# Gated attention, rms norm of a head's output: one fp32 product with ones, against two fp32r products with the high and low part of the sum

## What is computed

```python
o = o_intra + jnp.moveaxis(o_inter, 0, 1)
o = o * lax.rsqrt(jnp.mean(o * o, axis=-1, keepdims=True) + NORM_EPS)
o = o.reshape(B, L, D_INNER) * gn_g
return (o.astype(x.dtype) * jax.nn.silu(z)) @ w_out
```

## Time and profile before

| | |
|---|---|
| median of 3 runs | 1708.46 us |
| lowest, highest | 1706.99, 1709.57 us |
| the profiled execution's own time | 1711.55 us |
| its span | 1709.7 us |
| mean granted TensorE clock | 0.997 |
| PE busy | 1689.3 us (99%), 7852 matmuls |
| DVE, ACT, POOL busy | 960.2 (56%), 610.3 (36%), 976.4 us (57%) |

### The profile page before, as it was taken

How to read it: one execution, slowest core, us unless ns; L and a number is a source line. 1 busy time by engine, 2 the same in 40 slices (tenths; PEclk the granted TensorE clock), 3 DMA queues, 4 the chain that set the end, 5 groups by cost and what they waited for, 6 DMA issues and landing times.

```text
span 1709.7 us, 22074 instructions
## 1 busy us (share of the span) xinstructions
PE 1689.3 (99%) x7852; PEld 1404.5 (82%) x7852; DVE 960.2 (56%) x1637; ACT 610.3 (36%) x1160; POOL 976.4 (57%) x595
## 2 busy tenths in 40 slices
PE   9999999999999999998999999999999999999998
PEld 7788788888888888887888888888888888888887
DVE  6878422155642554255857444437657967775244
ACT  4455321243312222043733322322524037765022
POOL 6656566665667666665655466446564663333654
PEclk9999999999999999998999999999999999999999
DMA  5212232322233322323222222222232221111222
GB/s 205 85 58 79 87 99 98 99 87 91 95 101 108 99 98 93 104 99 102 84 89 72 77 96 87 83 77 87 86 99 81 90 96 50 50 50 62 87 89 84
DMA packets 52424, 152.26 MB, mean 89 GB/s; under 512 B 11376, under 2 KB 12528, under 8 KB 52336
## 3 DMA queue, kind: packets, MB, share of 16 engines
q1 hardware_dynamic: 51472, 149.50, 26.5%
q10 hardware_dynamic: 864, 1.57, 0.3%
HBM read 148.95 MB, written 2.10 MB: 88 GB/s over the span
## 4 chain that ended last, share of the span: by engine, by line
PE 94%; DVE 4%; issue 1%; ACT 1%; DMA 0%; SPq 0%; DVEq 0%; POOL 0%; ACTq 0%; POOLq 0%
PE bank L867 27%; PE bank L869 27%; PE bank L868 27%; DVE fx L2540 1%; PE bank L1714 1%; PE bank L1312 1%; PE bank L1313 1%; PE bank L1316 1%; PE bank L1557 1%; PE bank L1554 1%; PE bank L1553 1%; PE bank L1051 1%; PE bank L905 1%; PE bank L891 0%; DVE fx L2745 0%
## 5 line engine op out<-in xcount | busy, mean ns | idle before, releaser
L782 POOL TENSOR_SCALAR w_hi<-raw 128x1024 fp32r<-128x1024 f32 (+2 forms) x276 | 287.2, 1040 | 654.0 <-issue 482.9
L784 POOL TENSOR_TENSOR w_lo<-raw,w_hi 128x1024 fp32r<-128x1024 f32 (+2 forms) x276 | 646.7, 2343 | 23.1
L867 PE MATMUL bank<-op_hi,w_hi 128*128 128x512 f32 x964 | 381.8, 396 | 2.5 <-POOL w_lo L772 1.0
L869 PE MATMUL bank<-op_hi,w_lo 128*128 128x512 f32 x964 | 375.8, 390 | 0.0
L868 PE MATMUL bank<-op_lo,w_hi 128*128 128x512 f32 x964 | 375.5, 390 | 0.0
L867 PE MATMUL bank<-r,w_hi 128*128 128x512 f32 x856 | 339.2, 396 | 0.6 <-POOL w_lo L784 0.5
L869 PE MATMUL bank<-r,w_lo 128*128 128x512 f32 x856 | 333.9, 390 | 0.0
L868 PE MATMUL bank<-r,w_hi 128*128 128x512 f32 x856 | 333.7, 390 | 0.0
L867 PEld LDWEIGHTS bank<-op_hi,w_hi 128*128 128x128 f32 x964 | 181.4, 188 | 40.7 <-issue 2.0
L869 PEld LDWEIGHTS bank<-op_hi,w_lo 128*128 128x128 f32 x964 | 180.9, 188 | 38.0
L868 PEld LDWEIGHTS bank<-op_lo,w_hi 128*128 128x128 f32 x964 | 181.3, 188 | 36.3 <-issue 1.0
(11 more groups left out here) (306 smaller groups left out, 2346.5 us busy)
## 6 DMA issues: line engine op xcount, KB each, us to landing
raw<-in_weights SPq DMA_DIRECT2D x266, 512.0 KB, 3.3
out<-h SPq DMA_DIRECT2D x8, 256.0 KB, 2.0
h<-in_x SPq DMA_DIRECT2D x3, 512.0 KB, 8.3
raw<-in_weights SPq DMA_DIRECT2D x8, 192.0 KB, 2.4
raw<-in_weights SPq DMA_DIRECT2D x8, 128.0 KB, 2.7
cst<-in_consts SPq DMA_DIRECT2D x1, 832.0 KB, 11.4
raw<-in_weights SPq DMA_DIRECT2D x3, 256.0 KB, 3.2
rope_cos<-in_p ACTq DMA_DIRECT2D x3, 256.0 KB, 3.6
```

Of the source, the lines that this page charges most:

```text
L782: pool.tensor_scalar(hi, raw[:, r, at:w], 1.0, 0.0, ALU.mult, ALU.add).then_inc(hi_ready, 1)
L784: pool.tensor_tensor(lo, raw[:, r, at:w], hi.bitcast(F32), ALU.subtract).then_inc(split_ready, 1)
L867: pe.matmul(o, ah, bh, start=start, stop=False, skip_group_check=skip)
L869: return pe.matmul(o, al, bh, start=False, stop=stop, skip_group_check=skip)
```

## The change

After the last square is added up, ACT rounds the sum `acc` to fp32r (`oth`, into `total_hi`, which is tile 2 of `fx`) and DVE subtracts that from `acc` (`otl`, into `total_lo`, tile 0 of `fx`). `gla_sum` then makes two fp32r products with an fp32r matrix of ones, one with each part, added up in bank 7, instead of one fp32 product with `acc`. It waits for `otl` in place of `oacc2`. The matrix of ones in fp32r is made once by a copy of 128 x 128 on DVE, at the start of the stage `gla_a` (step `ones`), in the place of the constant `tri`, which nothing reads. On ACT `oth` stands behind the squares and the exponentials of the next head and ahead of `z3`, `z0` (heads 1 and 2) or right ahead of `osqrt` (heads 0 and 3). On DVE `otl` stands behind `on3` and `on0`, in every head.

```diff
+        total = nc.alloc_sbuf_tensor_at("total", [P, 3 * T], F32R, offset=nc.sbuf_base)
         fx = sb("fx", [P, 12, T], F32)
...
+        ones_r = nc.alloc_sbuf_tensor_at("ones_r", [P, P], F32R, offset=nc.sbuf_base + 4 * C0["tri"])[:, :]
         cst = sb("cst", [P, CONSTS], F32)
...
+        total_hi, total_lo = total[:, 2 * T:3 * T], total[:, 0:T]
...
-            gla_act += gla_decays_act(1, n) * inner + gla_names(p, *["z3", "z0"] * inner, "osqrt", "oh0", "oh3")
+            gla_act += gla_decays_act(1, n) * inner + gla_names(p, "oth", *["z3", "z0"] * inner, "osqrt", "oh0", "oh3")
...
-            gla_dve += gla_names(p, "on3", "on0", *["on1", "on2"] * first, "ors", "oz0", "oz3", "ol0", "ol3", *["on1"] * (not first), "oz1",
+            gla_dve += gla_names(p, "on3", "on0", "otl", *["on1", "on2"] * first, "ors", "oz0", "oz3", "ol0", "ol3", *["on1"] * (not first), "oz1",
...
             def gla_sum(p):
-                pe.wait_ge(d.sem, d.at(f"oacc2_{p}"))
                 pe.wait_ge(d.sem, d.at(f"on3_{p}"))
-                z.done(full_sum(7), f"osum_{p}")
+                pe.wait_ge(d.sem, d.at(f"otl_{p}"))
+                pe.matmul(ps[7][:, :], ones_r, total_hi, start=True, stop=False)
+                z.done(pe.matmul(ps[7][:, :], ones_r, total_lo, start=False, stop=True), f"osum_{p}")
...
+            def gla_total_high(p):
+                act.wait_ge(d.sem, d.at(f"oacc{GLA_BLOCKS[-1]}_{p}"))
+                hi(a, f"oth_{p}", total_hi, acc)
...
                 gla_squares(p)
                 if inner:
                     gla_decays(1, p + 1)
+                gla_total_high(p)
+                if inner:
                     gla_gate(3, p)
                     gla_gate(0, p)
                 gla_root(p)
...
+            d.done(dve.tensor_copy(ones_r, ones), "ones")
             d.done(dve.tensor_tensor_scan(later_keys, ones, ident, 1.0, ALU.mult, ALU.subtract), "later")
...
+            def gla_total_low(p):
+                sync(a, f"oth_{p}")
+                lo(d, f"otl_{p}", total_lo, acc, total_hi)
...
                 gla_gated(3, p)
                 gla_gated(0, p)
+                gla_total_low(p)
                 if first:
                     gla_gated(1, p)
                     gla_gated(2, p)
```

More of the change, by code:

```diff
@@ L458, in build @@
         stage("gla_a", 1, ["ah0", "ah1"] + [f"ab{m}" for m in M8] + ["ex0", "ex1", "ln0", "ln1"] + [f"{a}{m}" for a in ("ex", "ln") for m in range(2, KD)],
-              ["later", "sm", "al"] + [f"mn{m}" for m in M8] + QK, [f"a{m}" for m in range(KD - 1)])
+              ["ones", "later", "sm", "al"] + [f"mn{m}" for m in M8] + QK, [f"a{m}" for m in range(KD - 1)])
         def gla_names(p, *names):
```

## The result

The changed kernel takes 1714.96 us, median of 6 runs (1713.94 to 1715.64), the kernel before 1707.96 us in the 6 runs beside them. The ratio is 1.0037 (95% interval 1.0027 to 1.0047): slower by about 6.3 us (by the medians alone it would be 7.0). The profiled execution took 1715.55 us with a span of 1713.8, against 1711.55 and 1709.7 before.

A forecast was written before the change was run, and what follows sets the result against it. PE (TensorE), busy 99% of the span, was taken to bound the kernel. Savings of 0.41 us in heads 0 and 3 and losses of 1.95 in heads 1 and 2 gave +3.1: 1708.46 to 1711.6 us, range 1708.9 to 1716.7.

The forecast's parts named there:

- the mechanism that I gave 0.72: Four heads' sums: 0.41 us saved in heads 0 and 3, 1.95 us lost in heads 1 and 2, +3.1 us.
- one fall of 5.1 us: Behind a stall in head 1 or 2, PE's clock halves for 10.3 us and loses 5.1 us: 1716.7 us.
- The price of the products: Each head's sum on PE: two fp32r products take 0.46 us against 0.87 for fp32, saving 0.41 us without a wait.
- The step that laid the chain bare: Heads 1 and 2: PE's sum waits through gate 0, `z0`, `on0`, `otl`; stall about 2.4 us, net 1.95 us later.
- Where nothing should be late: `oth` off the chain, 2.0 us of cover in heads 0 and 3, nothing new late behind the stalls.
- The copy of ones: On DVE ahead of `later`: well under 1 us, costing nothing because DVE stands idle 5.92 us there.
- rival (b): Stalls in heads 1 and 2 halve PE's clock: 1716.7 us for one head, 1721.9 for both; chance 0.11.
- five waits of up to 1.1 us: Earlier PE waits in the trace that left the clock at 1.00, cited against a fall of the clock.
- The one fall in the trace: At 781.5 us PE's clock went from 1.00 to 0.50 for 10.3 us, after 3.3 us with 1.80 busy.
- The condition that I had set: Heads 1 and 2: the clock falls once 2.1 us without any product on PE is enough.
- Rival (a): All four heads' waits stay hidden: 0.41 us saved in each, -1.6 us, 1706.8 us; chance 0.08.
- Rival (c): The pair of products costs what one fp32 product did, 0.87 us: +4.7 us, 1713.2 us; chance 0.09.

The follow-up runs named there:

- The filled wait: Changed kernel with nine unread products of 128x512 in each of PE's two waits, heads 1 and 2: 1711.59 us, ratio 1.0018 to the kernel before.
- the fp32 sum: Changed kernel, waits and added steps included, but with one fp32 product as the sum in place of the pair: 1715.41 us, ratio 1.0044 to the kernel before.
- the one of one head: Changed kernel with the low part `otl` ahead of `on0` on DVE in head 2 alone: 1711.22 us, ratio 1.0013 to the kernel before.
- the first experiment: Changed kernel with the low part `otl` ahead of `on0` on DVE in every head: 1707.59 us, ratio 0.9993 to the kernel before.
- the sum behind gate 1: Changed kernel with PE's sum moved from ahead of gate 1 to behind it in heads 1 and 2: 1711.02 us, ratio 1.0014 to the kernel before.

## Why the prediction was right and wrong

The time lay in the range, and slower was the sign, but the mechanism that I gave 0.72 was only half of it: 3.1 us forecast, 6.3 measured. That the range held the time was in part luck: its upper end was one fall of 5.1 us, and what came was two falls of 1.7. Two falls at the price that I had put on them, 1721.9 us, would have lain outside.

- **The price of the products** was right: 0.46 us a pair and 0.42 saved where nothing waits, in heads 0 and 3. The 131 ns of the Trainium skill ("TensorE: Matmul & The Clock Gate", section "Back-to-back issue gap") would have been wrong here: products with N=512 are 0.23 us apart in the stream, before and after.
- **The step that laid the chain bare** was right in nearly each link. Predicted idle time about 2.1 us, measured 2.16; `z0` 0.04 us after the gate; `otl` in 0.68 us. Only the hand-over from `otl` (over at 982.11) to the sum (982.26) took 0.15 us, not 0.06. The filled wait measured this part alone at 3.1 us, the number of the forecast.
- **Where nothing should be late**, nothing was: `oth` was hidden, heads 0 and 3 had no wait, and no new wait came behind the stall. The copy of ones took 0.85 us and left DVE 5.78 us of the 5.92 that it had been idle.
- **The step that failed** is the weight of rival (b), that the stall brings the clock down: the sum priced a stall at its length alone. I gave the rival 0.11 because five waits of up to 1.1 us had left the clock alone. The one fall in the trace stood behind 3.3 us with little on PE, and the dense stream on both sides of the stall seemed to speak for the first. I should have split that evenly. Nor does the prediction say how those 3.3 us were made up:

```profile
780.22 1.05 PE L898 MATMUL bank<-cst,fx 128*128 128x1 f32 x8 [1.27 <-ACT fx L2157]
782.19 2.07 PE L905 MATMUL bank<-cst,st 128*128 128x128 f32 x8 [0.92 <-DVE st L3045]
786.57 0.77 PE L1312 MATMUL bank<-op_hi,w_hi 128*128 128x512 f32 x1 [2.30 <-ACT op_hi L1812]
```

  PE was idle for 1.5 of them, 1.27 us at a time at most, so the clock had fallen behind less idle time than the stall of 2.1 us that I forecast, though with small products between. And the 2.30 us, which the forecast passed over when it said that no idle time lay between 1.1 and 3.3, stood inside the low clock (781.5 to 791.8), so they could not speak for either side. The runs show where it lies here: 1.36 us twice and 1.6 us twice without a fall; 2.16 us with one in six of the seven profiled (both in the changed kernel's two profiles, one of two with the fp32 sum, the one of one head); 4.9 us with a longer one, twice. The condition that I had set, "2.1 us of nothing is enough", was met.
- **The size within that rival** was off the other way. I priced a fall at the 10.3 us of the earlier trace rows, 5.1 us lost; it was 3.42 us long and lost 1.7. Two of these make 3.4 us, and 3.1 + 3.4 = 6.5 us against 6.3 measured.
- Rival (a), hidden waits, describes the kernel of the first experiment, which only a swap on DVE makes. Rival (c) is refuted by the timeline of head 0.

A fall behind a wait agrees with the rule of the Trainium skill ("TensorE: Matmul & The Clock Gate", section "The HAM clock gate (the "warmup" mystery)") that activity is what releases the throttle: here 2.16 us without a product were followed by 3.41 us at 1.2 GHz in six of seven cases.

## What to carry to other kernels

Where an engine is the bound, a step put ahead of its instruction is priced by what stands before that step in its own engine's program: here 0.7 us of subtraction cost more because it stood behind a multiplication (`on0`) that waited for the unit that TensorE had only just finished, and a swap of two DVE steps took it off the path. Price a new stall of TensorE twice, by its length and by the low clock that may follow; if the trace has no stall of that length, give both cases real weight. Moving the waiting instruction back looks like the same cure but moves everything behind it too, and the sum behind gate 1 found its next wait 8 us later.

## What the runs showed that I had not expected

- A low clock can begin after TensorE is back at work: 0.6 us after it in head 1 of the changed kernel, 1.2 us in the run with one head, and it then stays for 3.42 us of full stream.
- Filling each of two waits with nine products of 0.227 us that nobody reads made the kernel 3.2 to 3.4 us faster than leaving them empty.
- Falls came in lengths of 3.41, 6.83 and 10.24 us. The one at about 780 us, where no run changes anything, was 10.24 us long in seven of the ten profiles and 6.83 in three, so the same code does not always lose the same time to the clock.
- A subtraction of 128x512 took 0.68 us alone, but the second of two took 2.71 us and ended 0.54 us behind POOL's work on a weight unit. The trace of the kernel before has the same: of 88 two-input steps of DVE with both inputs in SBUF that began while POOL was at such a unit, 70 ended 0.5 to 0.6 us behind POOL's end, whenever they had begun; of 429 with a bank as one input, none took over 0.76 us. That speaks for DVE waiting for POOL there; no run takes POOL's work away to show it. It goes the other way too: in the changed kernel `otl` (981.43) and POOL's low part (981.42) began together, `otl` took 0.68 us, and POOL 2.93 instead of the 2.40 of the kernel before. A little later, and `otl` might have been the one that waits; that was not tried.
